# Hybrid conv/pool block: conv matrices in 1 KB pieces with up to five buffers, and six tiles of the first phase transposed by DMA

## The reference, cut to what matters

```
u    = rms_norm(x, g1);  proj = u @ w_in           # 1024 -> 5120 columns
a, gate, p, gc, gp = split(proj)                   # each 1024 wide
conv = swish(layer_norm(depthwise31(a * sigmoid(gate)))) @ w_conv_out
pool = (trailing means of p, windows 2/4/8/16, minus p) @ pool_w * scale @ w_pool_out
h    = x + rms_norm((sigmoid(gc)*conv + sigmoid(gp)*pool) @ w_o, g2)
out  = h + rms_norm(square(relu(rms_norm(h, g3) @ w_ff1)) @ w_ff2, g4)
```

## Time and profile before

| | us |
|---|---|
| median of 3 runs | 972.39 (970.23 to 973.51) |
| the profiled execution's own time | 973.2 |
| its span on core 7, the slowest | 971.6 |
| PE busy / DVE / ACT | 947.4 / 405.3 / 326.8 |

### The profile page before, as it was taken

How to read it: one execution, slowest core, us unless ns; L and a number is a source line. 1 busy time by engine, 2 the same in 40 slices (tenths; PEclk the granted TensorE clock), 3 DMA queues, 4 the chain that set the end, 5 groups by cost and what they waited for, 6 DMA issues and landing times.

```text
span 971.6 us, 14273 instructions; the slowest of 8 cores (962.5 to 971.6 us)
## 1 busy us (share of the span) xinstructions
PE 947.4 (98%) x4990; PEld 479.7 (49%) x4990; DVE 405.3 (42%) x651; ACT 326.8 (34%) x592; POOL 42.4 (4%) x50
## 2 busy tenths in 40 slices
PE   5999999999989999999999999999999999999997
PEld 3555666775544444444444444444444444444444
DVE  3364232332647415675665541344323442333222
ACT  3565322111102492565544341133312341223211
POOL 3001000010110000010101000000000000000000
PEclk9999999999989999999999999999999999999999
DMA  9999602999999759569879994310242014210021
GB/s 193 217 218 177 77 1 46 138 155 144 126 121 177 131 123 148 112 143 234 152 195 177 201 177 109 98 65 1 66 127 93 19 26 116 96 47 1 1 87 66
DMA packets 125144, 111.69 MB, mean 115 GB/s; under 512 B 56945, under 2 KB 107377, under 8 KB 125074
## 3 DMA queue, kind: packets, MB, share of 16 engines
q0 software_dynamic: 55136, 46.45, 35.3%
q1 hardware_dynamic: 69792, 64.05, 25.7%
q10 hardware_dynamic: 146, 0.27, 0.1%
HBM read 127.78 MB, written 16.84 MB: 149 GB/s over the span
## 4 chain that ended last, share of the span: by engine, by line
PE 94%; DMA 4%; ACT 1%; issue 1%; DVE 0%; POOL 0%; DVEq 0%; ACTq 0%; POOLq 0%
PE ps L342 93%; DMA arena<-w_in 2%; DMA arena<-convw 2%; ACT arena L355 1%; PE ps L345 1%; ACT L355 0%; DVE arena L375 0%; POOL arena L378 0%; DVE arena L365 0%; DVEq L173 0%; ACT tmpA L355 0%; ACT junkb L355 0%; ACTq L140 0%; DVEq L140 0%; DVE sm L369 0%
## 5 line engine op out<-in xcount | busy, mean ns | idle before, releaser
L342 PE MATMUL ps<-arena 128*128 128x512 bf16 (+2 forms) x4560 | 916.8, 364 | 9.6 <-DMA arena<-convw 4.2
L342 PEld LDWEIGHTS ps<-arena 128*128 128x128 bf16 x4560 | 454.7, 104 | 464.3 <-issue 15.4
L355 ACT ACTIVATE tmpA<-ps 128x512 f32<-128x512 f32 x226 | 133.7, 595 | 343.2 <-PE ps L342 331.3
L358 DVE TENSOR_TENSOR arena<-tmpA 128x512 bf16<-128x512 f32 x128 | 88.2, 692 | 112.1 <-ACT tmpA L355 112.1
L358 DVE TENSOR_TENSOR arena<-ps,tmpA 128x512 bf16<-128x512 f32 x64 | 44.0, 691 | 151.8 <-ACT tmpA L355 133.5
L355 ACT ACTIVATE junkb<-ps 128x512 bf16<-128x512 f32 (+1 forms) x65 | 38.4, 591 | 177.5 <-DVE tmpA L358 112.7
L358 DVE TENSOR_TENSOR tmpA<-ps,gbt 128x512 f32<-128x512 f32 (+1 forms) x65 | 44.3, 681 | 34.3 <-PE ps L342 28.9
L355 ACT ACTIVATE junkb<-arena 128x1024 bf16<-128x1024 f32 (+1 forms) x33 | 34.6, 1050 | 60.6 <-DMA arena<-out 50.6
L358 DVE TENSOR_TENSOR sm<-sm 128x1 f32<-128x1 f32 x33 | 5.3, 160 | 108.5 <-ACT junkb L355 108.5
L355 ACT ACT_TABLE_LOAD x35 | 44.9, 1283 | 10.9 <-DVE mv L671 3.1
L355 ACT ACTIVATE arena<-ps 128x512 bf16<-128x512 f32 (+1 forms) x58 | 33.2, 586 | 36.2 <-PE ps L342 34.0
(11 more groups left out here) (40 smaller groups left out, 143.2 us busy)
## 6 DMA issues: line engine op xcount, KB each, us to landing
arena<-xh SPq DMA_DIRECT2D x32, 512.0 KB, 8.7
arena<-w_ff POOLq DMA_DIRECT2D x16, 1024.0 KB, 25.0
out<-arena SPq DMA_DIRECT2D x31, 512.0 KB, 3.0
arena<-out SPq DMA_DIRECT2D x28, 512.0 KB, 3.8
arena<-convw POOLq DMA_DIRECT2D x16, 768.0 KB, 13.0
arena<-w_in POOLq DMA_DIRECT2D x4, 1024.0 KB, 67.0
arena<-w_in POOLq DMA_DIRECT2D x2, 2048.0 KB, 22.6
arena<-w_in POOLq DMA_DIRECT2D x4, 512.0 KB, 20.3
```

The lines of the kernel that those rows point to most:

```text
L342: kb.op("pe", lambda e: e.matmul(out_ap, lhsT=lhsT, rhs=rhs, start=start, stop=stop, skip_group_check=skip), reads=reads, writes=writes)
L355: kb.op("act", lambda e: e.activation(out=out_ap, in_=in_ap, func=func, **kw), reads=reads, writes=writes)
L358: kb.op(eng, lambda e: e.tensor_tensor(out=out_ap, in0=in0, in1=in1, op=op), reads=reads, writes=writes)
```

## The change

Conv matrices: `wc_load` cuts its rows into pieces of 1 KB in place of 512 B. Two more buffers lie in the space of the second GLU weights, which is free after `glu(1, 15)`. Pieces 11 and 12 go into them, requested together before the first `gate_pool` group; pieces 13, 14 and 15 are requested when pieces 8, 9 and 10 are done, five ahead in place of three. `w_conv_out` still waits for piece 15.

First phase: `w_pool_out` is loaded as two halves, whose pieces are 1 KB in place of 2 KB. Tiles 10 to 15 are normalised into `tmpA` by a new function `a_norm_t`, which also issues a DMA transpose (128x1024) on SP; 48 products, 6 reads from PSUM by DVE, and the identity for these tiles fall away. Tile 10 is normalised at j = 7, tiles 11 and 12 at j = 8, tiles 13, 14 and 15 at j = 9, 10, 11. Since `tmpA` has four buffers, tile 14 waits for the transpose of tile 10, and tile 15 for that of tile 11.

SiLU: the four pairs come after `gate_pool` groups 22, 25, 28 and 30 in place of 23, 26, 29 and 31.

```
+        WC_OFF = [OFF_C + 4608, OFF_C + 7680, OFF_C + 10752, OFF_S + 8192, OFF_S + 11264]
+        Wc = [aview(o, 3072, g=8, d=3, n=128) for o in WC_OFF]
...
+        def a_norm_t(j):
+            n = ORDER.index(j)
+            k = next_k()
+            i = j % 4
+            src, sk = xs[:, n % 6, :], ("xs", n % 6)
+            ut = tmpA[:, i, :].bitcast(BF16)
+            ACT(junk[:, :], src, AF.Square, [sk], ["junkb", ("sm", k)], accum=sm[:, k:k + 1])
+            rs, rsk = rstd_col(128, k)
+            STT(ut, src, rs, gb[:, 0, :], ALU.mult, ALU.mult, [sk, rsk, ("gb", 0)], [("tmpA", i)])
+            DTR(uT[:, :, 128 * j:128 * j + 128], ut, [("tmpA", i)], [("ut", j)])
...
-        wload(S[2], wpo_v, [("w2", k) for k in range(8)])
+        wload(S[2][:, :, 0:512], wpo_v[:, :, 0:512], [("w2", k) for k in range(8)])
+        wload(S[2][:, :, 512:1024], wpo_v[:, :, 512:1024], [("w2b", k) for k in range(8)])
...
         for j in range(7, 16):
-            if j + 2 < 16:
-                a_norm(j + 2)
-            if j + 1 < 16:
+            if j == 7:
+                a_norm(9)
+                a_norm_t(10)
+            elif j == 8:
+                a_norm_t(11)
+                a_norm_t(12)
+            elif j + 4 < 16:
+                a_norm_t(j + 4)
+            if j + 1 < 10:
                 a_t(j + 1)
...
+        def wc_buf(w):
+            return {11: 3, 12: 4, 13: 2, 14: 0, 15: 1}.get(w, w % 3)
+
+        def cload(out_ap, in_ap, keys, after=()):
+            kb.op("pool", lambda e: e.dma_start(out=out_ap, in_=in_ap, max_dma_last_dim=2048), writes=keys, dma=True, after=after)
...
-            if q % 2 == 1 and w + 3 < 16:
-                wc_load(w + 3)
+            nw = w + (3 if w < 8 else 5)
+            if q % 2 == 1 and nw < 16:
+                wc_load(nw)
...
+        wc_load(11)
+        wc_load(12)
         interleave(groups[:12], side1, 3)
-        wload(S[1][:, :, :], wco_v, ["wco"], after=[kb.last_write[("Wc", 0)]])
+        wload(S[1][:, :, :], wco_v, ["wco"], after=[kb.last_write[("Wc", 1)]])
...
-            if n in (23, 26, 29, 31):
-                i = (n - 22) // 3
+            if n in (22, 25, 28, 30):
+                i = (n - 21) // 3
```

More of the change, by code:

```diff
@@ L209, in build_program @@
         UTt = [aview(OFF_C + b * 2304, 2304, g=16, m=144) for b in range(2)]
-        Wc = [aview(OFF_C + 4608 + b * 3072, 3072, g=8, d=3, n=128) for b in range(3)]
+        WC_OFF = [OFF_C + 4608, OFF_C + 7680, OFF_C + 10752, OFF_S + 8192, OFF_S + 11264]
+        Wc = [aview(o, 3072, g=8, d=3, n=128) for o in WC_OFF]
         wgc = aview(OFF_C, 8192, k=8, n=1024)
@@ L259, in build_program @@
             kb.disjoint([("UT", b), ("UTh", b)])
-        for b in range(3):
-            kb.reg(("Wc", b), (OFF_C + 4608 + b * 3072, 3072))
+        for b in range(5):
+            kb.reg(("Wc", b), (WC_OFF[b], 3072))
         kb.reg("wgc", (OFF_C, 8192))
@@ L630, in fold @@
                         MM(ps[:, b, :], pws[:, 2 * g + dk, i * 128:(i + 1) * 128], S[2][:, 2 * g + dk, hh * 512:(hh + 1) * 512],
-                           dk == 0, dk == 1, [("xb", g // 2), ("w2", 2 * g + dk)], [PSK(b)])
+                           dk == 0, dk == 1, [("xb", g // 2), ("w2", 2 * g + dk), ("w2b", 2 * g + dk)], [PSK(b)])
                     fold_ev.append((b, 2 * g + i, hh))
@@ L637, in build_program @@
         fold_ev = []
+        def wc_buf(w):
+            return {11: 3, 12: 4, 13: 2, 14: 0, 15: 1}.get(w, w % 3)
+        def cload(out_ap, in_ap, keys, after=()):
+            kb.op("pool", lambda e: e.dma_start(out=out_ap, in_=in_ap, max_dma_last_dim=2048), writes=keys, dma=True, after=after)
         def wc_load(w):
-            kb.op("pool", lambda e: e.dma_start(out=Wc[w % 3].rearrange("p g d n -> p (g d n)"), in_=convw[w // 2][:, (w % 2) * 3072:(w % 2 + 1) * 3072],
-                                                max_dma_last_dim=1024), writes=[("Wc", w % 3)], dma=True)
+            cload(Wc[wc_buf(w)].rearrange("p g d n -> p (g d n)"), convw[w // 2][:, (w % 2) * 3072:(w % 2 + 1) * 3072], [("Wc", wc_buf(w))])
         def cv_t2(cc):
@@ L652, in cv_mm @@
             w = cc * 2 + q // 2
+            wb = wc_buf(w)
             b = nb()
@@ L656, in cv_mm @@
                 for d in range(3):
-                    MM(ps[:, b, g4 * 128:(g4 + 1) * 128], UTt[bf][:, gl, 14 + d:142 + d], Wc[w % 3][:, gl % 8, d, :], d == 0, d == 2,
-                       [("UT", bf), ("UTh", bf), ("Wc", w % 3)], [PSK(b)])
+                    MM(ps[:, b, g4 * 128:(g4 + 1) * 128], UTt[bf][:, gl, 14 + d:142 + d], Wc[wb][:, gl % 8, d, :], d == 0, d == 2,
+                       [("UT", bf), ("UTh", bf), ("Wc", wb)], [PSK(b)])
             dst = ru[:, cc, :].rearrange("p (r g c) -> p g r c", r=16, g=16)[:, q * 4:q * 4 + 4, :, :]
```

## The result

| | before | after |
|---|---|---|
| median of 4 runs, us | 972.53 (970.23 to 973.51) | 1008.57 (1004.72 to 1009.24) |
| the profiled execution's own time | 973.2 | 1004.7 |
| its span on the slowest core | 971.6 (core 7) | 1003.2 (core 2) |

The change makes the kernel slower: ratio 1.0366, 95% interval 1.0334 to 1.0398. Forecast were 989 us and a range of 974 to 1001; the sign was right, the forecast loss was 19 us too small, and the time lies above the range. Medians and ratios here leave out the executions in which one half of the chip was disturbed, and where only such an execution has a trace, a core of the other half is shown.

A forecast was written before the change was run, and what follows sets the result against it. TensorE was taken as the bound (busy 947.4 of 971.6 us). 971.6 + 24.9 (first phase) - 7.0 (conv) - 1.0 (SiLU) = 988.5 us span, adjusted to a median of 989 us; range 974 to 1001.

The forecast's parts named there:

- The first phase: Tiles 10 to 15: transposes alternate one for one with weight packets, TensorE waits, `glu` begins at 120.4 us: +24.9 us.
- B: First phase: two transpose packets per weight packet, 4.8 us per tile, +12.3 us, together 976 us; chance 0.11.
- C: First phase: transposes packed many per turn keep ahead of TensorE, 2.2 us gained, 962 us median; chance 0.11.
- D: Conv stage: three matrices beside two transposes bring a 4 us wait, 996 us; chance 0.76 jointly with the main forecast.
- The clock: First phase: half clock after TensorE's waits put at 0, because tile 13 overlaps the next transpose; other end +2.8 us.
- SiLU: Output gate: pairs one `gate_pool` group earlier end the 0.96 us wait for ACT, -1.0 us; bounds 0 and -1.0.
- The conv matrices: Conv stage: earlier request ends matrix 14's wait and its half clock, -7.0 us; larger pieces 0, bounds 0 and +4.
- the data transposes: Conv stage: the transpose next in line to be late was taken to cost 0, between 0 and 2.4 us.
- The -7.0: Conv stage: TensorE's 4.2 us wait for matrix 14 plus 2.8 us lost to half clock afterwards, both removed.
- the upper end: Whole kernel: 1001 us, with tile 15 at 119 us, +2.8 for the clock and +4 in the conv stage.
- The end of the kernel: MLP to the end: nothing was forecast for this stretch.

The follow-up runs named there:

- the first experiment: Only the first-phase part (tiles 10 to 15 by DMA transposes, `w_pool_out` in halves) against the kernel before; conv and SiLU unchanged: 996.4 us, ratio 1.0260.
- the quiet kernel: First-phase part, with `w_pool_out` and the second GLU half requested only after tile 15's transpose, against the kernel before: 971.7 us, ratio 1.0005.

## Why the prediction was wrong, by its own steps

- **The first phase, right.** Forecast landings of tiles 10 to 15 were 75.2, 82.4, 89.6, 107.8, 113 and 115.5, with `pwf` at 100.6; read were 72.4, 79.2, 86.8, 105.9, 111.8 and 112.6, with `pwf` at 99.0. The steps of the transposes (6.8, 7.6, 6.8) are those of a pair at 106 to 119 ns against 112 forecast. The landings are 1.2 to 3.2 us earlier than forecast, because the last load of x landed at 65.7 us where I took 68. `pwf` was under-priced (12.3 us against 11.0), and 0.8 us of half clock are on the path (the clock, below). `glu` began at 120.0 against 120.4, so these errors nearly cancel, which is luck; the mechanism is not. The term came to +24.6 to +26.0 against +24.9. Its count of partners rightly had the conv matrices in 1 KB pieces, and these alone are 4.7 us of it, as the first experiment shows. Rivals B and C fall with the counts 2253 to 2249. The Trainium skill (DMA: Bandwidth & Descriptors, Queues, rings and completion order) has turns of 9 to 17 descriptors; equal counts exclude that only the transposes are packed so, as C had it, but not turns of equal length on both queues.
- **Rivals C and D.** The 2.2 us of C are nearly what the quiet kernel shows (1.9), for another reason than C's: without partners the transposes land in time. D named the place of the new waits, three matrices beside the transposes of groups 4 and 5, but the bunched requests with five buffers cost nothing in 512 B pieces (969.8 us), and in 1 KB pieces the conv part loses about 12 us with them and 14 without. So D had the place and not the cause.
- **The clock, right.** Granted clock around tile 13 (windows; length, busy by engine, PEclk, DMA share, GB/s):

```profile
105.00:109.00 4.00, 3.00 (x8) 1.08 (x9) 0.00 (x0) 0.00 (x0) 0.00 (x0) 0.50 1.23 194
109.00:113.00 4.00, 4.00 (x23) 1.87 (x22) 0.46 (x1) 1.19 (x2) 0.00 (x0) 0.72 1.28 210
```

  Half clock, 1.2 GHz, costs 1.5 + 1.1 = 2.6 us of work there, but tile 14's data landed at 111.8 and its products began at 112.54: 0.8 us of it are on the path, where I took 0.
- **SiLU, right:** -1.1 in the trace, as one edit 1.5 us by the runs.
- **The conv matrices, the step that failed.** I wrote that the larger pieces cost 0 "since the matrices no longer gate anything", and that the data transposes cost 0. Matrix 14 indeed no longer gates, though an earlier one does on core 2 (2.6 us). The transposes gate, and I had their price in hand and used it for the first phase alone. With 112 ns a pair from the earlier trace rows and 127 packets, a conv transpose beside 1 KB pieces takes 14.2 us, plus that of the one ahead. By itself this looks harmless beside the 14.5 us of the earlier trace rows; I never made the count for 512 B (75 ns, above), which gives 9.5 us and so 4 to 5 us of difference for each of the six transposes that run beside matrices. Measured, this size costs +14 us alone, and the whole part +12 where the term said -7.0: 19 us, as much as the miss, 1008.6 - 989.3. By the trace 14.0 us of it lie in the conv stage (+7.0 against -7.0), which is nearly all of what the span missed (1003.2 - 988.5 = 14.7). The profiled execution is 3.9 us under the median, and where the others lost that no trace shows.
- **The -7.0 itself** was too large also without the piece size: 1.3 us by the runs. I read the wait and the half clock of one core, while the time is that of the slowest of eight; the core next in line and the transpose behind the matrix (the earlier trace rows showed 2.4 us; 3.8 were found) keep most of it.
- **The range** had +4 us as the end for the conv stage, "one more wait like the removed one". That was a guess by likeness, not a bound, and even the upper end counted on all of the -7.0. With nothing for that term the end is 1008, and with the 8 us of two transposes in one queue in place of 4 it is 1012, which would have held the result. The sum of the upper end is not clean either: its terms give 989.3 + 3.5 + 2.8 + 4 = 999.6, and a full pair for tile 15 would put it at 122.2 us, not 119.
- **The end of the kernel** was put at nothing and cost 0.9 to 1.1 us (last section).

The profiled execution (1004.7) is the fastest of the four, so the tables of spans add to 31.6 us, while the medians differ by 36.0. The single parts, by their own runs, give 25.2 + 12 - 1.5 = 35.7; since the first two meet in the first phase, the agreement of the totals is better than that of the stages.

## What to carry to other kernels

Where two DMA queues share the engines, count packets, not bytes: here a stream of small packets advanced at one for each packet of its neighbour, or little more, so a larger piece on one queue is a tax on the other, and the traffic that gates the compute engine should have the small or no partners. Price a piece size by what else is under way in every stage where it is used, with the same rate that one stage has already shown. A late request is as good as a faster transfer only while it has slack: ask for bulk after the gating transfer, and check that the bulk is not next to be late.

## What the runs showed that was not expected

- A transpose of 128x1024 lands 4.6 us (median) after its issue with the weight queue empty, and 10.9 to 29.5 us after it in the changed kernel. The longest, of tile 13, stood behind `pwf`:

```profile
arena<-tmpA SPq DMA_TRANSPOSE x1, 29.5
```

- In the conv stage the exchange is not one for one all the time: 1068 transpose packets to 796 of the matrices before (1.34), 1494 to 1097 after (1.36). These are means of two kinds of stretches. Before, from 272 to 274 us, the counts are 392 to 398, and after, from 270 to 273, 411 to 430. In other stretches the transposes get 2.7 to 3.7 times as many, before (266 to 269 us) and after (278 to 284):

```profile
q1 hardware_dynamic: 783, 0.20, 110.3%
q0 software_dynamic: 210, 0.10, 28.2%
```
```profile
q1 hardware_dynamic: 946, 0.24, 96.2%
q0 software_dynamic: 349, 0.35, 34.3%
```

  There a transpose packet itself takes 1.103 x 3 x 16 / 783 = 68 ns before and 0.962 x 6 x 16 / 946 = 98 ns after, where it took 0.292 x 15 x 16 / 2249 = 31 ns in the first phase. The same matrices were exchanged one for one with transposes of 128x1024 (1445 to 1453, above), so it isn't the matrices alone. What makes these stretches stays open, and with it how much of the longer conv transposes is waiting for turns and how much is longer packets.
- On all eight cores the changed kernel needs 459.8 to 460.2 us from the first eviction of the MLP to its end, the kernel before 459.1, with the same time in between (453.4 us to the last eviction on the slowest core of each). The difference lies behind the last issue of an output, which lands 3.0 to 3.4 us after it in place of 2.1. All kernels with the first-phase part show it (+0.9 to +1.1 us on the mean), those with the conv part or SiLU alone show 0.1 us or less. Its cause stays open.
